# Twelve modulation tiles go into the diff attention, the hyena filter goes beside the mixer's first projection, and two feed-forwards pair their halves

## The reference

```python
# later block i
mod = cond @ ada_w[i] + ada_b[i]                     # 1024 x 6144
sh_a, sc_a, g_a, sh_f, sc_f, g_f = jnp.split(mod, 6, axis=-1)
h = modulate_2(rms_norm_2(x, norm_g[i, 0]), sh_a, sc_a)
# hyena of the first block, layer 1
filt_lat = hyena_filter(seq_lat, hf_w1[i], hf_b1[i], hf_freq[i], hf_w2[i], hf_b2[i], hf_w3[i])
y_hy_lat = hyena_mixer(p_lat[..., hy_cols], conv_d[i], filt_lat, hf_bias[i])
```

## Time and profile before

| | us |
|---|---|
| median of 3 runs | 3235.36 (3232.75 to 3237.53) |
| the profiled execution, its own time | 3237.39 |
| its span, from first to last instruction | 3234.2 |
| PE busy | 2805.7 (87%) |
| DVE, ACT busy | 1114.5 (34%), 958.2 (30%) |
| mean granted TensorE clock | 0.939 of full speed |

### The profile page before, as it was taken

How to read it: one execution, slowest core, us unless ns; L and a number is a source line. 1 busy time by engine, 2 the same in 40 slices (tenths; PEclk the granted TensorE clock), 3 DMA queues, 4 the chain that set the end, 5 groups by cost and what they waited for, 6 DMA issues and landing times.

```text
span 3234.2 us, 36185 instructions
## 1 busy us (share of the span) xinstructions
PE 2805.7 (87%) x14192; PEld 1782.8 (55%) x14192; DVE 1114.5 (34%) x1988; ACT 958.2 (30%) x1782; POOL 39.3 (1%) x51
## 2 busy tenths in 40 slices
PE   7998877777889668787778899898998989989898
PEld 3433422222455353222235788766998967875797
DVE  1751200001221420000014644446556455443655
ACT  2112211011121321000013544445444445443544
POOL 0010000000000000000000000000000000000000
PEclk9999999999899679999997999999999999998999
DMA  7672399999941017999990376573446406662152
GB/s 317 260 320 97 151 428 429 428 429 428 418 188 63 26 53 326 428 429 429 429 427 7 144 289 273 211 282 132 182 159 241 183 8 279 259 259 112 39 195 91
DMA packets 59486, 796.05 MB, mean 246 GB/s; under 512 B 8636, under 2 KB 9916, under 8 KB 10748
## 3 DMA queue, kind: packets, MB, share of 16 engines
q1 hardware_dynamic: 55664, 790.13, 59.5%
q10 hardware_dynamic: 3724, 4.59, 0.4%
HBM read 793.64 MB, written 1.05 MB: 246 GB/s over the span
## 4 chain that ended last, share of the span: by engine, by line
PE 67%; DMA 20%; DVE 6%; ACT 4%; issue 2%; SPq 0%; ACTq 0%; DVEq 0%; POOL 0%; POOLq 0%
DMA ring<-in_t_up 18%; PE banks L1796 11%; PE banks L1784 10%; PE banks L732 8%; PE banks L1391 8%; PE banks L866 5%; PE banks L881 4%; PE banks L1266 4%; DMA ring<-in_t_down 1%; PE banks L1513 1%; PE banks L656 1%; PE banks L1407 1%; PE banks L996 1%; PE banks L1610 1%; PE banks L1276 1%
## 5 line engine op out<-in xcount | busy, mean ns | idle before, releaser
L1391 PE MATMUL banks<-ring,arena 128*64 128x512 f32 x2048 | 482.0, 625 | 119.2 <-DMA ring<-in_t_up 64.1
L2684 DVE TENSOR_TENSOR ring_lo<-ring,w_hi 128x1024 fp32r<-128x1024 f32 x256 | 312.5, 1225 | 350.2 <-ACT w_hi L2121 350.2
L1391 PEld LDWEIGHTS banks<-ring,arena 128*64 128x64 f32 x2048 | 167.1, 144 | 432.4 <-issue 387.2
L2121 ACT CAST w_hi<-ring 128x1024 fp32r<-128x1024 f32 x256 | 267.6, 1052 | 391.5 <-PE banks L1796 196.7
L2315 DVE TENSOR_TENSOR arena<-arena,banks 128x512 f32<-128x512 f32 x32 | 22.0, 687 | 814.5 <-PE banks L1391 814.5
L1784 PE MATMUL banks<-u_hi,w_hi 128*128 128x256 f32 x1024 | 293.3, 286 | 5.0 <-DVE ring_lo L2684 4.1
L732 PE MATMUL banks<-arena,ring 128*128 128x512 f32 (+1 forms) x768 | 273.4, 517 | 20.7 <-ACT arena L696 13.4
L1784 PE MATMUL banks<-u_lo,w_hi 128*128 128x256 f32 x1024 | 289.6, 283 | 0.0
L1784 PE MATMUL banks<-u_hi,ring_lo 128*128 128x256 f32 x1024 | 289.6, 283 | 0.0
L1407 PE MATMUL banks<-ring,arena 128*64 128x512 f32 x1024 | 238.7, 621 | 34.9 <-DMA ring<-in_t_down 24.0
L1894 ACT COPY arena<-banks 32x512 f32 x96 | 55.3, 576 | 614.4 <-PE banks L1407 613.6
(11 more groups left out here) (346 smaller groups left out, 3700.4 us busy)
## 6 DMA issues: line engine op xcount, KB each, us to landing
ring<-in_t_ada SPq DMA_DIRECT2D x72, 2048.0 KB, 10.8
ring<-in_t_gate SPq DMA_DIRECT2D x64, 2048.0 KB, 17.1
ring<-in_t_up SPq DMA_DIRECT2D x64, 2048.0 KB, 17.3
ring<-in_t_down SPq DMA_DIRECT2D x64, 2048.0 KB, 17.3
ring<-in_t_ffn SPq DMA_DIRECT2D x64, 2048.0 KB, 12.1
ring<-in_t_ret_in SPq DMA_DIRECT2D x12, 2048.0 KB, 8.2
ring<-in_t_in_cd SPq DMA_DIRECT2D x6, 2048.0 KB, 8.5
ring<-in_t_sb_in SPq DMA_DIRECT2D x6, 2048.0 KB, 12.3
```

The lines of the kernel that those rows point to most:

```text
L1391: mm = nc.tensor.matmul(PS[64 * h:64 * h + 64, f.bank, :], x_cur[:, b, k, :], wview(un[h0 + h], KC)[:, k, :], start=(k == 0), stop=(k == K ...
L2121: nc.scalar.copy(w_hi[:, n % 4], w).then_inc(S("ffn_w_hi"), 1)
L2684: TT(w_lo, w, w_hi[:, n % 4].bitcast(F32), ALU.subtract).then_inc(S("ffn_w_lo"), 1)
```

## The change

Four edits are made together.

1. `plan_ada("b0", ...)` and all its calls go. The 12 tiles are planned after the attention's banks, on banks 6 and 7, and are made in the attention's loop: in an even step two, in an odd step one.
2. The norm of layer 1 and `hy_in` follow the combine directly. ACT issues the four DMAs of the hyena constants when the last combine fill is full, and no longer when it is free.
3. The filter's two sine layers and its third layer are made after units 0, 1 and 2 of `hy_in`, and its forward transform after them. On ACT the sines stand behind the eighth and twelfth evacuation of `hy_in`, on DVE the phase behind the convolutions of the first two units, and the decay behind the third.
4. In the feed-forwards of later blocks 1 and 3, `u_hi` and `u_lo` lie side by side, and high by high and high by low are one matmul of 512 columns. DVE adds the two bank halves and takes the Relu in the square's instruction. The up fills have four banks where they had two.

```diff
@@ plan
-            plan_ada("b0", 2, 0, 12, [4, 5, 6, 6])
...
+            shared = fills("da_shared", [6] * 16)
+            plan["da_out"] = [shared[4 * h + 3] for h in range(4)]
+            plan["b0_cols"] = [f for n, f in enumerate(shared) if n % 4 != 3]
+            fills("b0_rows", [7] * 12)
+            plan["b0_tiles"] = load(turn(12), units_of(a["t_ada"][2], *range(12)))
...
+        DA_TILES = [list(range(3 * (i // 2) + 2 * (i % 2), 3 * (i // 2) + 2 * (i % 2) + 2 - i % 2)) for i in range(8)]
@@ tensor
-                ada_pe("b0", hi=4)
...
+                norm_pe(pe, c, "cd_norm", 2)
+                beside = [lambda: hyena_mlp(0), lambda: hyena_mlp(1), hyena_tok]
+                dense_pe(pe, "hy_in", lambda i, q: uT[:, q, 0:N], N, 4, between=lambda i: beside[i]())
+                for f in plan["hf_tok"]:
+                    f.free.wait(pe)
                 forward(plan["hf_freq"], hf_tok)
-                ada_pe("b0", lo=8, hi=9)
-                norm_pe(pe, c, "cd_norm", 2, wait=False)
-                ada_pe("b0", lo=9)
-                u_ready(pe, c, 2)
-                dense_pe(pe, "hy_in", lambda i, q: uT[:, q, 0:N], N, 4)
...
                 for i in range(8):
                     if i < 7:
                         scores(i + 1)
+                    tiles = DA_TILES[i]
+                    ada_rows_pe(plan["b0_tiles"][tiles[0]], plan["b0_rows"][tiles[0]])
                     turn_probs(i)
+                    b0_cols(tiles[0])
+                    for t in tiles[1:]:
+                        ada_rows_pe(plan["b0_tiles"][t], plan["b0_rows"][t])
                     if i % 2:
                         out_head(i // 2)
+                    for t in tiles[1:]:
+                        b0_cols(t)
...
+                                if i in PAIRED:
+                                    nc.tensor.matmul(PS[:, f.bank, :], hi[:, q, :],
+                                                     u_pair[:, q].rearrange("p s t -> p (s t)"),
+                                                     start=(q == 0), stop=False, skip_group_check=True)
+                                    mm = nc.tensor.matmul(PS[:, f.bank, 0:N], lo[:, q, :], u_hi[:, q, :],
+                                                          start=False, stop=(q == KC - 1), skip_group_check=True)
+                                    continue
@@ scalar
-                plan["moe0_combine"][-1].free.wait(act)
+                plan["moe0_combine"][-1].full.wait(act)
                 act.dma_start(hy_const, a["k_hyena"]).then_inc(S("hy_const"), 16)
...
                 for i, f in enumerate(plan["hy_in"]):
                     copy_act(act, f, hy_p[:, i, 1:N + 1], PS[:, f.bank, 0:N])
+                    if i in (7, 11):
+                        act.wait_ge(S("hf_arg"), (i - 3) // 4)
+                        nc.scalar.activation(hf_x[0:64, :], hf_x[0:64, :], ACT.Sin).then_inc(S("hf_sin"), 1)
+                log_exp_tables()
...
                     if i < 7:
                         exps(i + 1)
+                    tiles = DA_TILES[i]
+                    if tiles[0] >= 2:
+                        plan["b0_cols"][tiles[0] - 2].full.wait(act)
+                    rows_act(plan["b0_rows"][tiles[0]], tiles[0] % 2, store=b0_store)
                     turn_act(i)
+                    for t in tiles[1:]:
+                        if t >= 2:
+                            plan["b0_cols"][t - 2].full.wait(act)
+                        rows_act(plan["b0_rows"][t], t % 2, store=b0_store)
@@ vector
+                    if g < 2:
+                        hyena_arg(g)
+                for t, f in enumerate(plan["hf_tok"]):
+                    f.full.wait(dve)
+                    TT(hf_tok[:, t, :], PS[:, f.bank, :], hy_decay[:, t, :], ALU.mult).then_inc(f.free.sem, 1)
...
                     if i < 7:
                         da_max(i + 1)
+                    if i >= 1:
+                        for t in DA_TILES[i - 1][1:]:
+                            b0_dve(t)
...
+                    b0_dve(DA_TILES[i][0])
...
+                plan["b0_cols"][-1].free.wait(dve)
+                gains_second(0)
                 residual_dve(ch, "cd_out", 1, 2, 1)
...
+                        if i in PAIRED:
+                            f.full.wait(dve, it)
+                            V_.tensor_copy(h, PS[:, f.bank, N:2 * N]).then_inc(S("ffn_low"), 1)
+                            dve.wait_ge(S("ffn_low"), 32 * PAIRED.index(i) + n - 3 + it * 8)
+                            TT(h, PS[:, f.bank, 0:N], h, ALU.add).then_inc(f.free.sem, 1)
+                            f.free.wait(dve, it)
+                            STT(h, h, 0.0, h, ALU.max, ALU.mult).then_inc(S("ffn_squared"), 1)
```

More of the change, by code:

```diff
@@ L507, in block_program @@
             fills("da_turn", [4, 5] * 4)
-            fills("da_out", [6, 7] * 2)
+            shared = fills("da_shared", [6] * 16)
[3 more added lines that the diff above has]
+            plan["b0_tiles"] = load(turn(12), units_of(a["t_ada"][2], *range(12)))
+            for u, f in zip(plan["b0_tiles"], plan["b0_rows"]):
+                u.used = f.full
             fills("da_sub", [4, 5] * 2)
@@ L601, in block_program @@
         w_hi = region_r("w_hi", 8192, [4, KC, P])
[L602 removed]
+        u_pair = region_r("u_pair", 12288, [KC, 2, N])
+        u_hi, u_lo = u_pair[:, :, 0, :], u_pair[:, :, 1, :]
         y_tok = region(W + 2048, [TC, D])
@@ L1449, in _, with hyena_mlp @@
             if LAST >= 3:
-                ada_pe("b0", hi=4)
-                pe.wait_ge(S("hy_const"), 64)
-                for r in range(2):
+                def hyena_mlp(r):
                     f = plan["hf_mlp"][r]
@@ L1461, in _, with hyena_tok @@
                     mm.then_inc(f.full.sem, 1)
-                    ada_pe("b0", lo=4 + r, hi=5 + r)
-                pe.wait_ge(S("hf_sin"), 2)
-                for t in range(TC):
-                    f = plan["hf_tok"][t]
-                    f.open(pe)
-                    nc.tensor.matmul(PS[:, f.bank, :], hf_x[0:64, t * P:(t + 1) * P], hf_w3[0:64, :],
-                                     start=True, stop=True).then_inc(f.full.sem, 1)
-                ada_pe("b0", lo=6, hi=8)
-                for f in plan["hf_tok"]:
-                    f.free.wait(pe)
+                def hyena_tok():
+                    pe.wait_ge(S("hf_sin"), 2)
+                    for t in range(TC):
+                        f = plan["hf_tok"][t]
+                        f.open(pe)
+                        nc.tensor.matmul(PS[:, f.bank, :], hf_x[0:64, t * P:(t + 1) * P], hf_w3[0:64, :],
+                                         start=True, stop=True).then_inc(f.full.sem, 1)
                 def forward(fill_list, src):
@@ L1933, in _ @@
                 act.dma_start(hf_w3[0:64, :], a["hf_w3"][0]).then_inc(S("hy_const"), 16)
-                ada_act("b0", hi=4)
-                for r in range(2):
-                    act.wait_ge(S("hf_arg"), r + 1)
-                    nc.scalar.activation(hf_x[0:64, :], hf_x[0:64, :], ACT.Sin).then_inc(S("hf_sin"), 1)
-                    ada_act("b0", lo=4 + r, hi=5 + r)
-                log_exp_tables()
-                ada_act("b0", lo=6, hi=8)
-                for q, f in enumerate(plan["hf_freq"]):
-                    copy_act(act, f, hf_F[:, q, :], PS[:, f.bank, :])
-                ada_act("b0", lo=8, hi=9)
-                stat_act(act, c, [(hT[:, k, :], None) for k in range(KC)], plan["cd_norm"][0], 2 * N)
+                marks = [f.free for f in plan["moe0_combine"][KC:]]
+                stat_act(act, c, [(hT[:, k, :], marks[k]) for k in range(KC)], plan["cd_norm"][0], 2 * N)
                 rsqrt_act(act, c, plan["cd_norm"][0], 2 * N, D)
-                ada_act("b0", lo=9)
                 shift_act(act, c, 1, 0, 2)
@@ L2128, in ffn_act @@
                     ffn_hi(i, n, it)
-                    if 4 <= n < 12:
+                    if 4 <= n < 12 and i not in PAIRED:
                         f = plan[p + "up"][n - 4]
@@ L2413, in _, with hyena_arg @@
             if LAST >= 3:
-                ada_dve("b0", 2, 0, hi=3)
-                for r in range(2):
+                norm_dve(dve, c, "cd_norm", 1, 0, 2)
+                def hyena_arg(r):
                     f = plan["hf_mlp"][r]
@@ L2421, in _ @@
                     trig(hf_x[0:64, :], hf_k[0:64, :], 64, False).then_inc(S("hf_arg"), 1)
-                    ada_dve("b0", 2, 0, lo=3 + r, hi=4 + r)
-                for t, f in enumerate(plan["hf_tok"]):
-                    f.full.wait(dve)
-                    TT(hf_tok[:, t, :], PS[:, f.bank, :], hy_decay[:, t, :], ALU.mult).then_inc(f.free.sem, 1)
-                ada_dve("b0", 2, 0, lo=5, hi=8)
-                norm_dve(dve, c, "cd_norm", 1, 0, 2)
-                ada_dve("b0", 2, 0, lo=8)
-                gains_second(0)
                 orig = [4, 5, 6, 7, 8, 9, 10, 11, 0, 1, 2, 3]
```

24 lines of the change are left out of this document (17 added, 7 removed).

## The result

The changed kernel took **3196.9 us** (median of 4 runs, 3193.89 to 3197.35) against 3234.38 for the kernel before on the same chip (4 runs, 3232.75 to 3237.53): ratio 0.9881 [0.9864, 0.9898], 37.5 us less. The forecast was 3203, 32 less. The profiled execution took 3197.1 (span 3194.8, granted clock 0.949).

What follows compares the result with a forecast made beforehand. The chain that ended last was 67% PE and 20% DMA, so edits had to remove PE work or waiting. Terms -39.1 + 13.8 - 6.8 = -32.1 gave a median of 3203 us; own range 3196 to 3213, wider range 3190 to 3227.

Steps and rivals of the forecast that it cites:

- The first step: Experts' combine to hyena projection: with tiles and filter moved away, the projection starts at 865.1, not 920.9; gain 55.8 us.
- the second: Filter made beside the hyena projection: 16.7 us paid (15.7 to 22) for its matmuls, handovers and forward transform.
- The third: Modulation tiles in the diff attention's loop: cost 13.8 us (3.5 to 37), loop 78.0 at a clock of about 0.8.
- the fourth: Feed-forwards of blocks 1 and 3: 512 merged matmuls save 13 ns each, gain 6.8 us (0 to 6.8).
- rival (b): Diff attention keeps the higher clock, so its tiles cost only 3.5 us: total 3193 us; chance 0.13.
- The sign of being wrong: Ahead of the projection: the norm's statistic starting later than 848 would show the forecast wrong.
- the all-high case: Diff attention with tiles, wholly at the higher clock: even step 8.85, odd step 8.0, loop 67.7 us.
- rival (a): Diff attention stays at the lower clock throughout, so its tiles cost 37 us: total 3226 us; chance 0.11.
- Rival (c): Filter's chain stretched beside the projection, both sines 10 us late, so the moving gains little: total 3223 us; chance 0.06.
- Rival (d): Attention's tiles 6 to 11 arrive late, each holding PE 9.36 us, 56 in all: total 3259 us; chance 0.04.

## Why the prediction was right, and where its terms were off

The first step holds in its mechanism and its size, the second in its mechanism and nearly in its size. The third had the wrong clock, and the fourth was priced too high. That the total came out near 3203 is partly luck: errors of 10 us and 5 us offset each other, and 3196.9 lies at the lower edge of the forecast's own range (3196 to 3213), nearer to rival (b)'s 3193.

**The way to the projection** was right: 56.0 against 55.8. Its parts hold too: 3.85 us of idling ahead of the statistic by the DMA issues, 1.7 for the lower clock in it (9.23 against 7.49, granted 0.83 against 1.00; forecast 1.5). The sign of being wrong, a statistic later than 848, came true by the letter (849.07), but only since the combine ended 1.9 later: the squares began 3.1 us behind it, where the forecast had 3.5. What the forecast took as given, that the issues must lie on ACT's way, the run with SP's issues shows to be a choice, worth 3.7 us by the trace and 4.9 by the medians.

**The filter beside the projection** cost 18.5 against 16.7, inside its bounds. The wait ahead of the second layer is 2.28 (forecast 2.2), and from the projection's last matmul to the transposes it is 13.9 (forecast 13.3). What was left out is the first unit of the projection, which took 1.2 more than in the kernel before, since PE idles 8.58 us ahead of it. And the forward transform took 8.76, at a granted clock of 0.81 behind 3.3 us of waiting (forecast 7.03 and 1).

**The tiles in the attention** is the step that failed in its number: 3.8, where 13.8 was taken. The working of the all-high case was right (a pair 16.6 us against 16.85 forecast, the loop 68.0 against 67.7). What failed is "so I take the nearest row, about 0.8": the clock was 0.83, 1.00, 1.00 and 0.90 over the four pairs, and even the first and last lost only single groups. So what came is rival (b)'s time for this term. The two runs on the gap show why. With rows in the gap the clock was 0.81 to 1.00, even with no transposes and a third of the tiles gone, and then the loop is 10.5 us shorter than the old one (53.7 against 64.2); with the rows behind the turn it is 0.80 to 0.85. So the forecast's 0.8 is about what the same work gets with the gaps left open. The term is thus -10.5 for the gaps filled and the clock that this gives back, and +14.3 for what stands outside them. The forecast had priced the old loop at its own clock and the new one as a mean of two, and did not ask what the filling of each gap does to the old work.

By the Trainium skill's sentence as the prediction applied it (TensorE: Matmul & The Clock Gate, Part 4: PE-mode transpose), rival (a) would have come. The loop has 12 groups of a tile's transposes and 8 of the turn's, and was granted 1.00 over two whole pairs, with PE busy for 12.49 us of 16.6. No run here takes the transposes away from a loop at the lower clock, so the rule itself is neither shown nor refuted; it doesn't decide this loop. The prediction's support for it was misread: of the 20.62 us of busy PE in the row at 0.50, only 2.80 are transposes.

**The paired halves** gave 3.3 in their own matmuls against 6.8 (6.6, if the prediction's rows are taken to three digits). The term was mis-sized: 13 ns for a merged pair came from two groups of one width each. Where 512 and 256 alternate, a 512 costs 0.236, not 0.227, in nearly all rounds, a chunk 0.353, and a merge saves 0.240 + 0.120 - 0.353 = 7 ns. The 13 ns came only in the first round of block 3 (a chunk 0.347). DVE didn't hold PE up, as forecast; but the working "1.15 + 5 x about 0.42 = 2.8 to 3.1" gives 3.25, and DVE came out at 2.83 since it has four operations beside the split and not five. What no term had is the granted clock of the last block's attention, some 4 us in the traces, which goes with this edit. The Trainium skill's figure (TensorE: Matmul & The Clock Gate, section "Wait — 56ns, not 53.3ns?") would give an estimated 1.3, below the 3.3 of the trace.

**The rest.** Rival (c) is out: the waits for the two sines were 2.28 and 0.77, where 2.2 and 0.95 were forecast. Rival (d) is out: no DMA wait in the attention. The errors of the terms are: the attention 10.0 better than forecast, the pairing's own matmuls 3.5 and the filter 1.8 worse, and the median of before 1 lower than the one shown.

## What to carry to other kernels

Independent work is worth most where it fills an idle gap that recurs in a loop. Price it as two changes: the gap that it fills, and the granted clock that all the loop's old work then gets; here PE waits 12 us less in the loop, and its old work takes about 14 us less (some 24 in place of 38.4), which together nearly pay for some 30 us of tiles. Work that covered a wait in its old place must be looked at together with that wait: without the tiles, the filter in front of the norm cost 10.7 us more than beside the projection. And a chain that passes between engines beside a projection belongs early enough that matmuls of the projection are left to cover each handing over, the last one included: the run with the earlier links had no wait in front of any of them. Last, compare the stretches that no edit touches too: here one of them held some 4 us.

## What the hardware showed that was not expected

- The attention loop with PE busy 12.49 us of 16.6 was granted a clock of 1.00 for two pairs; the old one, busy 9.43 of 16.60, was granted 0.60; and the loop with its gaps open again, busy for 64.7 us of 99.7, 0.80 to 0.85.
- Matmuls of 512 columns cost 0.227 us in the down groups, 0.230 in runs of eight, and 0.236 between matmuls of 256; those of 256 cost 0.120, 0.119 and 0.117. One alternating pair cost 0.353 in most rounds and 0.347 in a few first ones, at the same granted clock.
- The same 217 matmuls of the last block's latent attention took 73.8 us in both traces without the pairing and 70.0 to 70.1 in the ten with it, at a granted clock of 0.81 and 0.85, though the pairing stands in other stages. The cause is open.
